# A state-space stage on one Trainium2 core: the scan loop by pairs of units, with GpSimd's part of it moved to VectorE

## The reference, cut to what matters

```python
def _s5_direction(u_g, a_re, a_im, bb_re, bb_im, c_re, c_im, reverse):
    bu_re = jnp.einsum('lgc,gpc->lgp', u_g, bb_re)
    bu_im = jnp.einsum('lgc,gpc->lgp', u_g, bb_im)
    ar = jnp.broadcast_to(a_re, bu_re.shape)
    ai = jnp.broadcast_to(a_im, bu_re.shape)
    _, _, h_re, h_im = lax.associative_scan(
        _complex_linear_combine, (ar, ai, bu_re, bu_im), reverse=reverse, axis=0)
    ...
    return jnp.einsum('lgp,gcp->lgc', h_re, cr) - jnp.einsum('lgp,gcp->lgc', h_im, ci)
...
y = y_fwd + y_bwd + d_skip * u
y = gelu(y)
y = y * sigmoid(y @ w_glu + b_glu)
```

## Time and profile before

| | us |
|---|---|
| time, median of 3 runs | 2251.73 |
| lowest and highest of them | 2250.52, 2251.89 |
| span of the profiled execution | 2252.9 |
| PE busy in the span | 1870.8 |
| DVE busy in the span | 1500.0 |
| POOL busy in the span | 1018.6 |
| ACT busy in the span | 414.4 |

### The profile page before, as it was taken

How to read it: one execution, slowest core, us unless ns; L and a number is a source line. 1 busy time by engine, 2 the same in 40 slices (tenths; PEclk the granted TensorE clock), 3 DMA queues, 4 the chain that set the end, 5 groups by cost and what they waited for, 6 DMA issues and landing times.

```text
span 2252.9 us, 22858 instructions
## 1 busy us (share of the span) xinstructions
PE 1870.8 (83%) x6912; PEld 1133.1 (50%) x6912; DVE 1500.0 (67%) x2341; ACT 414.4 (18%) x879; POOL 1018.6 (45%) x862
## 2 busy tenths in 40 slices
PE   6988788888899999997797798777777777777776
PEld 5977466566668988653353354232323232222222
DVE  5545999999994553656556566667666666666654
ACT  4332222222224343111011011000100000100001
POOL 2042666666661510344344345344444555555332
PEclk9998789998899999999999999999999999999999
DMA  4432122222224555899999999999999999999997
GB/s 163 169 106 100 38 80 85 76 79 82 84 93 150 183 183 199 344 421 421 417 417 417 400 398 406 422 421 422 414 421 421 419 421 422 422 422 422 421 422 301
DMA packets 92552, 659.13 MB, mean 293 GB/s; under 512 B 10288, under 2 KB 10288, under 8 KB 12976
## 3 DMA queue, kind: packets, MB, share of 16 engines
q0 software_dynamic: 73728, 536.90, 57.6%
q1 hardware_dynamic: 18752, 121.36, 14.8%
HBM read 656.13 MB, written 2.10 MB: 292 GB/s over the span
## 4 chain that ended last, share of the span: by engine, by line
PE 36%; DMA 29%; DVE 19%; issue 10%; POOL 3%; ACT 1%; DVEq 1%; POOLq 0%; ACTq 0%; SPq 0%
DMA uv<-u_tab,eid 29%; PE ps L1405 12%; DVE hs L885 4%; DVE hs L893 3%; PE ps L1212 3%; PE ps L1116 3%; PE ps L1118 3%; PE ps L1117 3%; PE ps L1355 2%; POOL uv L425 2%; DVE uv L1056 2%; DVE pb L877 1%; PE ps L1338 1%; PE ps L1339 1%; DVE pa L875 1%
## 5 line engine op out<-in xcount | busy, mean ns | idle before, releaser
L1405 PE MATMUL ps<-uv,dg 128*128 128x512 f32 x2048 | 958.7, 614 | 268.5 <-DVE dg L1062 261.1
L1056 DVE CUSTOM_DVE_ANT_0 uv<-uv,xn 128x2048 f32<-128x2048 f32 x256 | 586.9, 2293 | 381.0 <-DMA uv<-u_tab,eid 353.2
L1405 PEld LDWEIGHTS ps<-uv,dg 128*128 128x128 f32 x2048 | 379.7, 193 | 825.3 <-issue 465.4
L425 POOL DMA_INDIRECT uv<-v_tab,eid x256 | 268.4, 1048 | 611.0 <-PE ps L1405 351.5
L422 POOL DMA_INDIRECT uv<-u_tab,eid x256 | 340.1, 1328 | 201.6 <-issue 184.5
L653 ACT ACTIVATE ga<-av 128x1 f32<-128x1 f32 x256 | 51.9, 203 | 1186.5 <-DVE av L1056 1186.5
L1212 PE MATMUL ps<-hT,ring 128*128 128x256 f32 x1024 | 263.8, 415 | 0.0
L1212 PEld LDWEIGHTS ps<-hT,ring 128*128 128x128 f32 x1024 | 207.7, 208 | 55.9 <-issue 24.7
L705 DVE TENSOR_TENSOR low_ring<-ring,wh 128x2048 fp32r<-128x2048 f32 x43 | 107.2, 2497 | 76.6 <-ACT wh L444 76.5
L1062 DVE TENSOR_SCALAR dg<-prm,ga,gw 128x128 f32<-128x128 f32 x256 | 94.0, 367 | 66.3 <-ACT ga L653 32.6
L1270 PE MATMUL ps<-hs,cp 128*32 128x256 f32 x256 | 76.0, 425 | 66.7 <-DVE hs L901 66.6
(11 more groups left out here) (245 smaller groups left out, 2342.0 us busy)
## 6 DMA issues: line engine op xcount, KB each, us to landing
ring<-W SPq DMA_DIRECT2D x104, 1024.0 KB, 4.8
uv<-u_tab,eid POOLq DMA_INDIRECT x256
uv<-v_tab,eid POOLq DMA_INDIRECT x256
xn<-x SPq DMA_DIRECT2D x2, 1024.0 KB, 6.4
bwt<-bw SPq DMA_DIRECT2D x8, 256.0 KB, 4.8
cwt<-cw SPq DMA_DIRECT2D x8, 256.0 KB, 5.0
out<-xn SPq DMA_DIRECT2D x4, 512.0 KB, 5.2
keyt<-keys SPq DMA_DIRECT2D x1, 1024.0 KB, 7.5
```

The lines of the kernel that those rows point to most:

```text
L425: pool.indirect_dma_start(uv[:, s, 1, :], None, v_tab, at).then_inc(s_vv[s], 16)
L1056: nc.vector.tensor_tensor_reduce(uv[:, j % UV, 0, :], uv[:, j % UV, 0, :], xn[:, T, :], 1.0, 0.0, ALU.mult, ALU.add, av[:, hh, j:j + 1]).t ...
L1405: ins = nc.tensor.matmul(ps[:, 4 * T + n, :], dg[:, j % 2, :], uv[:, j % UV, 1, n * 512:(n + 1) * 512], start=False, stop=last and i == 2 ...
```

## The change

VectorE takes two units at once, those of the same direction from neighbouring groups of 32 input rows, so a turn is a pair and there are eight pairs a body (`PPL`) and four a chunk (`PPC`). The work stays; only its instructions and places change:

- `input_products` takes 2 x 2 x 272 = 1088 elements at once, from banks 2 to 5 together; there is no second set of banks.
- GpSimd's three steps are VectorE's: `turned_inputs` adds and subtracts over 544 elements in place in `pa`, `scans` runs four scans of 272 in place in `pa`, `turned_back` multiplies by the cosine and by the sine, 1024 elements each, and `real_parts` makes both parts, 512 elements each. `out_matrices` is VectorE's too, with its six instructions of 256 elements a chunk.
- `angles` works over 544 elements, and rounds what ScalarE has written into `tb`, with an addition of MAGIC (before it multiplied iota again).
- ScalarE's absolute value, sine and cosine take 544 elements at once; `turns` is two instructions a pair.
- TensorE's matmuls are the same in number and size. Those of the two units of a pair alternate. Its turn t is: half a gate tile, `state_inputs(t-1)`, `state_outputs(t-3)`, the other half of the gate tile; gate tiles are two pairs late (`LAG = 2`).
- VectorE's turn t: `scalars` at a chunk's start, input products of t-2, both parts of t-3, `turned_inputs` and scans of t-2, `take_y` where one is due, the angles of t, `turned_back(t-2)`, `inputs_low` at a chunk's start, and one part of `out_matrices` in the first three turns of a chunk.
- `pa` and `pb` are single, `oc`, `os_` and `trig` double by pairs.

The diff, cut to its core:

```diff
-        LAG = 4
-        RPL = 2 * SPC
+        LAG = 2
+        PPL = SPC
+        PPC = SPC // 2
...
+        def place(t):
+            return t // PPC, t % 2, t % PPC // 2
+        def units(t):
+            cc, way, jp = place(t)
+            return slice(4 * jp + way, 4 * jp + way + 3, 2)
...
-                    sp.wait_ge(s_bu, SPC * (2 * b + cc) + 8)
+                    sp.wait_ge(s_bu, PPC * (2 * b + cc) + PPC)
...
-            def scan_body(b, first=False):
-                for t in range(RPL):
-                    if t >= 1 or not first:
-                        turn_inputs(*behind(b, t, 1))
-                    if t >= 2 or not first:
-                        turn_back(*behind(b, t, 2))
-                    if t % SPC < 3:
-                        out_matrices(b, t // SPC, t % SPC)
...
-                nc.scalar.activation(tb[:, t % 2, :], iota, ACT.Copy, scale=scur[:, cc, 0, t % SPC:t % SPC + 1]
+                at = units(t).start
+                nc.scalar.activation(tb[:, t % 2, 0, :], iota, ACT.Copy, scale=scur[:, cc, 0, at:at + 1])
+                nc.scalar.activation(tb[:, t % 2, 1, :], iota, ACT.Copy, scale=scur[:, cc, 0, at + 2:at + 3]
                                      ).then_inc(s_tb, 1)
-                nc.scalar.activation(ang[:, t % 2, 1, :], ang[:, t % 2, 0, :], ACT.Abs).then_inc(s_abs, 1)
+                nc.scalar.activation(trig[:, s, 0, :, :], ang[:, s, :, :], ACT.Abs).then_inc(s_abs, 1)
+                nc.scalar.activation(trig[:, s, 1, :, :], ang[:, s, :, :], ACT.Sin, scale=-TWO_PI).then_inc(s_trg, 1)
...
             def angles(b, t):
-                nc.vector.tensor_scalar(tb[:, 2, :], iota, scur[:, t // SPC, 0, t % SPC:t % SPC + 1], MAGIC,
-                                        ALU.mult, ALU.add).then_inc(s_vl, 1)
+                nc.vector.tensor_scalar(rnd[:, :, :], tb[:, s, :, :], MAGIC, None, ALU.add).then_inc(s_rnd, 1)
+                dve.wait_ge(s_rnd, n + 1)
+                nc.vector.scalar_tensor_tensor(ang[:, s, :, :], rnd[:, :, :], MAGIC, tb[:, s, :, :],
                                                ALU.subtract, ALU.subtract).then_inc(s_ang, 1)
             def input_products(b, t):
+                s, n = t % 2, PPL * b + t
                 dve.wait_ge(s_trg, 2 * n + 2)
+                dve.wait_ge(s_bu, n + 1 + PPL)
+                dve.wait_ge(s_os, n + 2)
+                bu = ps[:, 2:6, 0:L].rearrange("p (u r) t -> p u r t", u=2)
+                nc.vector.tensor_tensor(pa[:, :, :, :], bu, turn(0), ALU.mult).then_inc(s_ab, 1)
+                nc.vector.tensor_tensor(pb[:, :, :, :], bu[:, :, ::-1, :], turn(1), ALU.mult).then_inc(s_ab, 1)
+            def turned_inputs(b, t):
+                dve.wait_ge(s_ab, 2 * n + 4)
+                nc.vector.tensor_tensor(pa[:, :, 0, :], pa[:, :, 0, :], pb[:, :, 0, :], ALU.add).then_inc(s_gin, 1)
+                nc.vector.tensor_tensor(pa[:, :, 1, :], pa[:, :, 1, :], pb[:, :, 1, :], ALU.subtract).then_inc(s_gin, 1)
             def scans(b, t):
+                for k in range(2):
+                    dve.wait_ge(s_gin, 2 * n + 1 + k)
+                    for u in range(2):
+                        r = scur[:, cc, 1, at + 2 * u:at + 2 * u + 1].broadcast_to([P, L])
+                        nc.vector.tensor_tensor_scan(pa[:, u, k, :], r, pa[:, u, k, :], 0.0, ALU.mult, ALU.add
+                                                     ).then_inc(s_gst, 1)
+            def turned_back(b, t):
+                s, n, kept = t % 2, PPL * b + t, slice(0, SEQ) if t % 2 else slice(META, L)
+                dve.wait_ge(s_gst, 4 * n + 4)
+                dve.wait_ge(s_y, n - 1 + PPL)
+                nc.vector.tensor_tensor(oc[:, s], turn(0), pa[:, :, :, kept], ALU.mult).then_inc(s_oc, 1)
+                nc.vector.tensor_tensor(os_[:, s], turn(1), pa[:, :, :, kept], ALU.mult).then_inc(s_os, 1)
             def real_parts(b, t):
+                dve.wait_ge(s_oc, n + 3)
+                dve.wait_ge(s_os, n + 3)
+                nc.vector.tensor_tensor(oc[:, s, :, 0, :], oc[:, s, :, 0, :], os_[:, s, :, 1, :], ALU.subtract
                                         ).then_inc(s_re, 1)
+                nc.vector.tensor_tensor(oc[:, s, :, 1, :], oc[:, s, :, 1, :], os_[:, s, :, 0, :], ALU.add
+                                        ).then_inc(s_im, 1)
+            def pair(b, t, first=False):
+                if t >= 2 or not first:
+                    input_products(*behind(b, t, 2))
+                if t >= 3 or not first:
+                    real_parts(*behind(b, t, 3))
+                if t >= 2 or not first:
+                    turned_inputs(*behind(b, t, 2))
+                    scans(*behind(b, t, 2))
...
             def state_inputs(b, t):
                 pe.wait_ge(s_ab, 2 * n + 2)
+                for r in range(2):
+                    for part in range(3):
+                        for u in range(2):
+                            rows = slice(32 * (2 * jp + u), 32 * (2 * jp + u) + 32)
+                            w = (bwL if part == 2 else bwH)[rows, cc, way, r, :]
+                            x = uP[rows, cc, part % 2, :]
...
+                            ins = nc.tensor.matmul(ps[:, 2 + 2 * u + r, 0:L], w, x, start=(part == 0), stop=(part == 2))
                 ins.then_inc(s_bu, 1)
             def scan_body(b, first=False):
+                for t in range(PPL):
+                    gated_now = t >= LAG + 1 or not first
+                    if gated_now:
+                        half_gate(*behind(b, t, LAG), 0)
+                    if t >= 1 or not first:
+                        state_inputs(*behind(b, t, 1))
                     if t >= 3 or not first:
                         state_outputs(*behind(b, t, 3))
+                    if gated_now:
+                        half_gate(*behind(b, t, LAG), 1)
```

More of the change, by code:

```diff
@@ L547, in scan_body @@
                         cos_sin(*behind(b, t, 1))
-                    if t % SPC == 0:
-                        inputs_high(b, t // SPC)
-                    if t % 2 and (t >= LAG + 2 or not first):
-                        gate(*behind(b, t, LAG + 2))
+                    if t % PPC == 0:
+                        inputs_high(b, t // PPC)
+                    if t >= LAG + 1 or not first:
+                        gate(*behind(b, t, LAG + 1))
             scan_body(0, first=True)
@@ new lines, in scans @@
+            def scans(b, t):
+                n, cc = PPL * b + t, t // PPC
+                at = units(t).start
+                for k in range(2):
[4 more added lines that the diff above has]
+                                                     ).then_inc(s_gst, 1)
@@ L910, in take_y @@
                                                ).then_inc(s_ye, 1)
-            def scan_body(b, first=False):
-                for t in range(RPL):
-                    if t % SPC == 0:
-                        scalars(b, t // SPC)
-                    angles(b, t)
-                    if t >= 1 or not first:
-                        input_products(*behind(b, t, 1))
-                    if t % SPC == 0:
-                        inputs_low(b, t // SPC)
-                    if t >= 2 or not first:
-                        scans(*behind(b, t, 2))
-                    if t >= 3 or not first:
-                        real_parts(*behind(b, t, 3))
-                    if t >= 2 or not first:
-                        cos_products(*behind(b, t, 2))
-                    if t == SPC + 4:
-                        take_y(b, 0)
-                    if t == 4 and not first:
-                        take_y(b - 1, 1)
+            def pair(b, t, first=False):
[6 more added lines that the diff above has]
+                    scans(*behind(b, t, 2))
+            def scan_body(b, first=False):
+                for t in range(PPL):
+                    if t % PPC == 0:
+                        scalars(b, t // PPC)
+                        if first and t == 0:
+                            angles(b, t)
+                            inputs_low(b, 0)
+                    pair(b, t, first)
+                    if t == PPL - 1:
+                        take_y(b, 0)
+                    if t == PPC - 1 and not first:
+                        take_y(b - 1, 1)
+                    if not (first and t == 0):
+                        angles(b, t)
+                    if t >= 2 or not first:
+                        turned_back(*behind(b, t, 2))
+                    if t % PPC == 0 and not (first and t == 0):
+                        inputs_low(b, t // PPC)
+                    if t % PPC < 3:
+                        out_matrices(b, t // PPC, t % PPC)
             scan_body(0, first=True)
@@ L934, in _ @@
                 scan_body(b)
-            input_products(*behind(BODIES, 0, 1))
             for t in range(2):
-                scans(*behind(BODIES, t, 2))
-                real_parts(*behind(BODIES, t, 3))
-                cos_products(*behind(BODIES, t, 2))
+                pair(BODIES, t)
+                turned_back(*behind(BODIES, t, 2))
```

(15 more changed lines are left out.)

209 lines of the change are left out of this document (78 added, 131 removed).

## The result

The changed kernel takes 2182.65 us, the median of 4 runs (2177.77 to 2183.18), against 2251.81 us (2250.52 to 2252.78) for the kernel before beside it: a ratio of 0.9688, 95% interval 0.9674 to 0.9702, 69.2 us less. The prediction was 2169 with a range of 2152 to 2206.

What follows compares the result with a forecast made beforehand. VectorE, held up by GpSimd, was taken to bound the state-space stage. 32 pairs at 11.74 us make 375.7 us; a gain of 84.6, taken as 82.5, brings the 2252.9 us span to 2170.4, 2169 as a time, range 2152 to 2206.

Steps and rivals of the forecast that it cites:

- What sets the stage: State-space stage: VectorE bounds it, its instructions with two SBUF operands standing still while GpSimd runs; 7.19 us a unit.
- The price of a pair: VectorE's loop: undisturbed instructions of a pair sum to 10.80 us, 11.74 with its share of a chunk's extras.
- Whole durations: Rival for VectorE's loop: no instruction starts before the last ends; 12.77 us a pair, 2202 us in all; chance 0.13.
- A pair thus 11.14 us: TensorE's work for a pair at full clock, from 5.57 us a unit; off the path with 0.6 us to spare.
- Its clock above 0.97: Sign of being right in the profile after: TensorE's clock above 0.97, its waits for input products and real parts short.
- the very wait hidden: TensorE's `state_inputs` waiting for banks 2 to 5: about 7 us of cover hides it; without cover 2 us a pair.
- A clock with dips in each chunk: Sign of being wrong, listed beside VectorE idle before the input products, a bound by TensorE; no size given.
- clock rival: TensorE becomes the bound through its falling clock: 2210 us, or 2182 with half the loss; chance 0.18.
- The tail: End of the stage: GLU product starts 2.55 us after `take_y`, at 594.5 us; a lower clock there costs about 2 us.
- The sum 84.6 - 2: Total gain: 84.6 us up to TensorE's GLU product, less about 2 us for its clock, taken as 82.5 us.
- the three outcomes that are faster: VectorE stays the undisturbed bound, 2169 us, chance 0.62; whole durations, 2202 us, 0.13; TensorE bound through its clock, 0.18.
- the two slower ones: TensorE's clock low for most of the loop, 2490 us, chance 0.04; long rows belonging to shapes, far slower, 0.01.

Runs made afterwards that it cites:

- gpsimd_narrow: Kernel before the change, with GpSimd's instructions in the three looped bodies cut to 8 or 16 elements, leaving work out: 2179.2 us.
- gpsimd_busy: Changed kernel, with GpSimd also multiplying a scratch tile of 128x384 eight times a pair, nobody waiting for it: 2280.5 us.
- round_on_scalar: Changed kernel, with the rounding of the angles moved from VectorE to ScalarE: 2158.8 us (4 runs), ratio 0.9587 to the kernel before.
- split_units: Changed kernel, with ten of VectorE's instructions a pair cut in two, one for each unit, same elements: 2188.0 us.
- one_unit_after_other: Changed kernel, with TensorE's input and output matmuls of a pair's first unit before those of the second, not alternating: 2182.8 us.
- pad_96: Changed kernel, with 96 increments of an unused semaphore on VectorE right behind the scan loop: 2171.3 us (4 runs), ratio 0.9633 to the kernel before.

## Why the prediction was right, and where its terms were off

**What sets the stage: right, shown.** VectorE was the bound, and the long durations came from GpSimd (gpsimd_narrow, gpsimd_busy). It is still the bound with the rounding moved, at 99% of the loop (round_on_scalar).

**The price of a pair: right.** 10.71 us against 10.80. The sums of 1.20, 0.60, 0.63, 0.62 and 1.13 hold to 0.01 us; the rounding cost 0.44 and not 0.52. The stage took 378.7 us against 379.3: 0.09 us a pair and 0.7 at the head came in cheaper (6.2 us to the first input products instead of 6.95), and about 3 us went to VectorE's short waits, for `ucur` (2.0), `tb` (1.1) and others, to which I had given no term.

**Whole durations: fell.** L853 starts 1.20 us after L852, which lasts 1.28. The one neighbour in the timeline that does wait for the one before it, L840 for L838, starts 0.03 us after its end. The Trainium skill, page "VectorE: DVE Perf Modes", section "The DRAIN you can't avoid", has an exception that the prediction left out: an operation that is not held starts before the pipe of the one ahead is empty. The trace agrees with the exception, and split_units prices an instruction at 0.066 us beside its elements.

**TensorE: the conclusion right, two of its numbers wrong.** "A pair thus 11.14 us" doubled one unit. The matmuls of two units use different groups of 32 rows or columns, and a pair takes 7.2 (gate) + 1.0 + 1.1 = 9.3 us in the timeline above. The Trainium skill, page "TensorEngine Tiling (Array Packing)", section "Key Properties", lets such tiles run in parallel; the rows agree. I had read the rows as sequential, and so gave TensorE 0.6 us to spare where it has some 2. "Its clock above 0.97" and short waits for the input products were wrong too: behind waits of up to 3.1 us for the input banks the clock falls, to a mean of 0.95 and 0.93 in two windows of the loop (330 to 425 and 425 to 520 us). I had called the very wait hidden, which it is for VectorE; for TensorE's clock it is not. A clock with dips in each chunk stood among the signs of a bound by TensorE; the dips came, some two a chunk, and VectorE stayed the bound, so that sign was badly chosen. The two errors meet: the dips cost nothing since the spare time is larger. By the clock rival's arithmetic these means lose 0.6 to 0.8 us a pair, which with 11.14 us makes 11.7 to 11.9, at or over the 11.6 us that VectorE took: an estimate, which no run tests. That the conclusion held is in this part luck.

**The tail: right, but the clock's part varies.** The GLU product starts 2.48 us after `take_y`, against 2.55. Of the 2 us for the clock 1.5 are there: its 128 matmuls take 29.3 us, against 27.8 in before, and over its first 5 us the granted clock is 0.71. Windows of after, and of before at the same event:

```profile
591.20:596.20 5.00, 5.00 (x17) 4.18 (x18) 2.29 (x1) 2.10 (x2) 0.00 (x0) 0.71 0.01 3
```

```profile
679.10:684.10 5.00, 5.00 (x25) 4.39 (x24) 2.29 (x1) 3.56 (x3) 0.00 (x0) 1.00 0.58 210
```

At the start of the merge, 33 us after `take_y`, it is the other way round. The clock falls in before, and not in this execution of after; windows of before, of after, and of one_unit_after_other:

```profile
708.90:712.90 4.00, 3.90 (x20) 3.91 (x21) 0.00 (x0) 0.00 (x0) 0.00 (x0) 0.57 0.53 221
```

```profile
622.60:626.60 4.00, 3.99 (x33) 3.99 (x34) 0.00 (x0) 0.00 (x0) 0.00 (x0) 1.00 0.55 231
```

```profile
626.30:630.30 4.00, 3.92 (x20) 3.92 (x21) 0.00 (x0) 0.00 (x0) 0.00 (x0) 0.57 0.54 225
```

So up to the end of the output projection the profiled execution is again 0.9 us ahead of before, 217.3 against 218.2. Eight of the ten kernels built from after have the fall at the merge and lose more in the GLU product (30.4 to 30.9 us), and take 219.9 to 220.3: 2.6 to 3.0 us more. With a stage that begins 2.0 us later (212.0 us in one_unit_after_other) this is most of the 4.9 us by which the profiled execution stands below the median.

**What had no term: the experts, +10.8 us.** I took everything behind the stage as unchanged. The sum 84.6 - 2 missed the two additional fetch stops that came with VectorE's changed program. Without them the kernel is 11 us faster (pad_96), at 2171.3, 2 us from the forecast. The range held the time, as it had room for dearer instructions and a slower clock; what filled it was neither, so that the range held is partly luck.

The chances don't add up exactly: the three outcomes that are faster make 0.93 and the two slower ones 0.05, where the prediction has 0.94 and 0.04.

## What to carry to other kernels

Compare the shortest and the longest duration of one instruction on one shape: where they differ, look up what ran beside the long ones, and price the work at the short one plus the elements that have to come over. Where a neighbouring engine's instructions block yours, work moved onto the bound engine can pay, as can moving a small step to a third engine that doesn't block it. When a stretch with a loop that the edit doesn't touch gets slower, look at what follows the loop's branch, compare the instruction packets in the DMA queues, and pad the program, before looking for a cause in the data flow.

## What the runs showed of the hardware

- A hardware loop of VectorE stopped for 5.4 to 5.6 us at each turn back while 8 KB of instructions came in, with nothing but "issue" beside it. 52, 96 or 99 semaphore instructions far ahead of the loops took two of four stops away, and the kernel became 11 us faster with 96 and with 99 of them. With 52, in a single run, it was 18 us below the median of after, 13 below the profiled execution, which has the same short start and tail.
- The matmuls of two units on other groups of 32 rows or columns overlapped almost fully: eight output matmuls in the time of four, even when they were issued unit by unit.
- TensorE's clock went to a mean of 0.67 over 4 us after a wait of 2.9 us (346.39 us in after); ahead of the earlier trace rows it had waited 4.2 us.
- VectorE's scans, products and sums with two SBUF operands stretched beside GpSimd's instructions (256 elements from 0.39 to 0.91 us, 544 from 0.71 to 1.34), those with a PSUM operand did not (1088 elements, 1.28 us in both).
